# One layer of a hybrid decoder on one core: V of the first token chunk computed in the carry block, transfers issued in earlier or later blocks, and the next chunk's inputs loaded in eight pieces

## What is computed

```
h = rmsnorm(x)
[q | k | v | u | g_att | g_s5] = h @ w_in
att = rmsnorm(diff_attention(q, k, v)) * (1 - lambda_init)      # 8 heads, causal
s5  = y + d * u, y from the diagonal complex recurrence on u   # 64 groups, 64 states each
z   = gelu(s5);  s5o = z * sigmoid(z @ w_glu + b_glu)
x   = x + (sigmoid(g_att) * (att @ w_proj_att) + sigmoid(g_s5) * (s5o @ w_proj_s5)) @ w_out
x   = x + PEER(rmsnorm(x))      # per token 8 heads pick 16 of 16384 experts by top-k
y   = rmsnorm(x)
```

## Time and profile before

| What | Value |
|---|---|
| Runs, median (lowest to highest) | 4465.69 us (4462.35 to 4467.46) |
| The profiled execution's own time | 4462.64 us |
| Its span in the trace | 4460.9 us |
| Its mean granted TensorE clock | 0.908 of full speed |
| PE busy | 3361.5 us, 75% |
| DVE busy | 3039.5 us, 68% |
| ACT busy | 1502.3 us, 34% |
| POOL busy | 1323.9 us, 30% |
| Moved by DMA | 1416.84 MB, mean 318 GB/s |
| of it expert rows gathered by POOL | x1056, queue q0, 1129.94 MB |
| L911 POOL gathers | 1248.5 us |
| L1014 DVE dot products | 1288.9 us |
| L656 PE stationary tiles | 1109.4 us |

### The profile page before, as it was taken

The page is one execution under the profiler, slowest core; times in us unless marked ns, Lnnn a source line. Parts: engine busy times, 40 slices in busy tenths (PEclk is TensorE's granted clock), DMA queues, the critical chain, the costliest instruction groups (busy, mean ns, idle before and its releaser), DMA issues. The chain is left out here.

```text
span 4460.9 us, 43476 instructions
## 1 busy us (share of the span) xinstructions
PE 3361.5 (75%) x13280; PEld 1915.9 (43%) x13280; DVE 3039.5 (68%) x6500; ACT 1502.3 (34%) x3882; POOL 1323.9 (30%) x1168
## 2 busy tenths in 40 slices
PE   7857979787768869877668758877777777777776
PEld 4646666544434444344456634432222222222221
DVE  6473021788888878877776758886676676666664
ACT  2121140333553324254443323223333333333332
POOL 0100000233223333322233323344444444444442
PEclk9878989998879889988888969999999999999999
DMA  3117425998778999966699979899999999999997
GB/s 130 18 3 105 146 86 179 369 394 340 261 271 347 362 383 392 409 211 228 221 364 402 405 266 417 327 412 419 419 418 416 412 413 413 412 412 400 411 407 304
DMA packets 284909, 1416.84 MB, mean 318 GB/s; under 512 B 47459, under 2 KB 88899, under 8 KB 147587
## 3 DMA queue, kind: packets, MB, share of 16 engines
q0 software_dynamic: 159344, 1129.94, 63.5%
q1 hardware_dynamic: 124946, 283.98, 18.7%
q10 hardware_dynamic: 384, 0.13, 0.0%
HBM read 1370.00 MB, written 42.11 MB: 317 GB/s over the span
## 5 line engine op out<-in xcount | busy, mean ns | idle before, releaser
L911 POOL DMA_INDIRECT arena<-in_uv,arena x1056 | 1248.5, 1182 | 2312.9 <-DVE arena L1024 1417.6
L1014 DVE CUSTOM_DVE_ANT_0 arena<-arena 128x1024 f32<-128x1024 f32 x1056 | 1288.9, 1222 | 510.4 <-DMA arena<-in_uv,arena 481.9
L1132 PE MATMUL ps<-arena 128*128 128x512 f32 (+1 forms) x2288 | 1086.6, 620 | 404.3 <-ACT arena L1101 404.3
L656 PE MATMUL ps<-arena 128*128 128x256 f32 (+2 forms) x3456 | 1109.4, 481 | 146.6 <-DMA arena<-in_w_stat 68.3
L656 PEld LDWEIGHTS ps<-arena 128*128 128x128 f32 x3456 | 682.7, 201 | 536.9 <-issue 354.1
L1132 PEld LDWEIGHTS ps<-arena 128*128 128x128 f32 (+1 forms) x2288 | 413.4, 190 | 1076.9 <-ACT arena L1101 629.1
L1024 DVE SCALAR_TENSOR_TENSOR arena<-arena 128x1024 f32<-128x1024 f32 x484 | 618.9, 1279 | 18.7 <-ACT arena L1091 18.7
L1082 ACT ACTIVATE arena<-arena 128x2 f32<-128x2 f32 x528 | 107.2, 203 | 1533.1 <-DVE arena L1014 1514.8
L1091 ACT ACTIVATE arena<-arena 128x1 f32<-128x1 f32 x1056 | 253.4, 287 | 17.7 <-ACT arena L1082 0.5
L1082 ACT ACT_TABLE_LOAD x156 | 200.1, 1283 | 46.0 <-PEq L1260 28.9
L1101 ACT ACTIVATE arena<-ident,arena 128x128 f32<-128x128 f32 x540 | 187.2, 394 | 8.8
(11 more groups left out here) (251 smaller groups left out, 3294.7 us busy)
## 6 DMA issues: line engine op xcount, KB each, us to landing
arena<-in_w_stat SPq DMA_DIRECT2D x216, 512.0 KB, 7.8
arena<-in_cache_k SPq DMA_DIRECT2D x64, 512.0 KB, 10.7
arena<-in_cache_v SPq DMA_DIRECT2D x64, 512.0 KB, 11.5
arena<-in_w_mov SPq DMA_DIRECT2D x14, 2048.0 KB, 14.5
arena<-in_uv,arena POOLq DMA_INDIRECT x1056, 13.1
arena<-in_x SPq DMA_DIRECT2D x16, 512.0 KB, 9.2
arena<-scr_s POOLq DMA_DIRECT2D x64, 128.0 KB, 12.9
scr_s<-arena SPq DMA_DIRECT2D x16, 384.0 KB, 15.2
```

Of the source, the lines that this page charges most:

```text
L656: last = nc.tensor.matmul(ps[:, bank, 0:w], wbuf[m % NWB][:, kc * P:(kc + 1) * P], moving[:, kc, :], start=(kc == 0), stop=(kc == KC - 1))
L911: pool.indirect_dma_start(ring[s % RING], None, dr["uv"], bass.IndirectOffsetOnAxis(ap=idx[:, g % 4, j:j + 1], axis=0)).then_inc(row_in[s ...
L1014: nc.vector.tensor_tensor_reduce(ring[s % RING][:, 0:D], ring[s % RING][:, 0:D], h2r[:, b % 2, :], 1.0, 0.0, ALU.mult, ALU.add, act_in[:, ...
L1132: last = nc.tensor.matmul(ps[0:m, 4 * (b % 2) + c, :], diag[:, n % 4, 0:m], ring[s % RING][:, D + 512 * c:D + 512 * (c + 1)], start=start, ...
```

## The change

- The loads of the u weights are issued at the end of the norm block instead of the start of the next one.
- The seven Toeplitz copies are issued at the start of the carry block instead of the end of the block before. PE waits for them ahead of the samples' outputs.
- V of the first chunk (tokens 0 to 255) is computed in the carry block: SP loads its columns of `hT` back from `scr_h` and the V weights in two halves, the second behind `zs_ready`, since its place holds the samples' z until then. PE does the products behind L522, ACT copies them out, SP stores them, and ACT waits for these stores before the first gelu of the late block. `stage_values` runs for chunks two and three only, and "s5" of the first chunk loads no V weights.
- In the late block DVE's copy of the samples' z stands first instead of behind the states, SP's store of it stands ahead of the samples' states, and the first three weight tiles are issued at the block's start instead of behind the sixth z store.
- `stage_queries` loads the next chunk's z and `hT` in eight pieces of two feature blocks each, two pieces at each of heads 1 to 4, ahead of that head's store of scores, instead of two DMAs at head 2.

```diff
@@ norm block, SP
+                for k in range(2):
+                    sp.dma_start(slab[:, k, :, :].rearrange("p a b -> p (a b)"), dr["w_mov"][k]).then_inc(slab_in[k], 16)
@@ parameter block, SP
-                for k in range(2):
-                    sp.dma_start(slab[:, k, :, :].rearrange("p a b -> p (a b)"), dr["w_mov"][k]).then_inc(slab_in[k], 16)
...
-                sp.wait_ge(toe_zero, 2)
-                for s in range(1, ST8):
-                    sp.dma_start(m_toe[s * CH:(s + 1) * CH, :, s * CH:P],
-                                 kst[:, :, 0:ST8 - s, :].rearrange("p g t c -> p g (t c)")).then_inc(toe_in, 16)
@@ carry block
+        h_v0 = lay(AT_KS + 1664, [KC, 2 * P])
+        w_v0 = [lay(AT_KS + 1664 + 2 * D, [KC, 512]), lay(AT_WS, [KC, 512])]
+        v_st0 = lay(AT_KS + 1664 + 2 * D, [2, D])
-        zs_st = lay(AT_WS + G * P + 256, [KC, NS])
+        zs_st = lay(AT_WS, [KC, NS])
@@ carry block, PE
                 last.then_inc(zs_ready, 1)
+                pe.wait_ge(se_free, GP)
+                for k in range(2):
+                    pe.wait_ge(v0_in[k], 32 - 16 * k)
+                    for b in range(2):
+                        for kc in range(KC):
+                            last = nc.tensor.matmul(ps[:, 2 * k + b, :], h_v0[:, kc, b * P:(b + 1) * P], w_v0[k][:, kc, :],
+                                                    start=(kc == 0), stop=(kc == KC - 1))
+                        last.then_inc(v_ready, 1)
@@ carry block, ACT
+                act.wait_ge(v_ready, 2)
+                for k in range(2):
+                    for b in range(2):
+                        act.wait_ge(v_ready, 2 * k + b + 1)
+                        nc.scalar.activation(v_st0[:, b, 512 * k:512 * (k + 1)], ps[:, 2 * k + b, :], ACT.Copy).then_inc(v_free, 1)
@@ carry block, SP
+                for s in range(1, ST8):
+                    sp.dma_start(m_toe[s * CH:(s + 1) * CH, :, s * CH:P],
+                                 kst[:, :, 0:ST8 - s, :].rearrange("p g t c -> p g (t c)")).then_inc(toe_in, 16)
+                sp.dma_start(h_v0, scr_h.rearrange("p (c t) -> p c t", c=KC)[:, :, 0:2 * P]).then_inc(v0_in[0], 16)
+                for k in range(2):
+                    if k:
+                        sp.wait_ge(zs_ready, 1)
+                    sp.dma_start(w_v0[k].rearrange("p a b -> p (a b)"), dr["w_mov"][2 + k]).then_inc(v0_in[k], 16)
+                sp.wait_ge(v_free, 4)
+                for b in range(2):
+                    sp.dma_start(out["v"][b * P:(b + 1) * P, :], v_st0[:, b, :]).then_inc(v_out[b], 16)
                 sp.wait_ge(rec, N_CARRIED)
@@ late block, SP
+                for m in range(NWB):
+                    load_tile(sp, m)
+                sp.wait_ge(zs_free, 1)
+                sp.dma_start(z_all[:, :, SEQ:T], zs_st).then_inc(zs_out, 16)
                 sp.wait_ge(rec, N_LATE + 8)
...
                     if c == KC - 3:
                         sp.wait_ge(yp_ready, KC)
-                        for m in range(NWB):
-                            load_tile(sp, m)
                         load_hT(sp, 0)
@@ stage_merge, SP
-                        if j in (4, 8):
+                        if j in (4, 8) and (c or fold):
@@ stage_queries, SP
-                        if h == 2 and c + 1 < len(CHUNKS):
-                            load_zT(sp, c + 1)
-                            load_hT(sp, c + 1)
+                        if 1 <= h <= 4 and c + 1 < len(CHUNKS):
+                            for part in (2 * h - 2, 2 * h - 1):
+                                load_next(sp, c + 1, part)
@@ the loop over chunks
-            stage_values(c)
+            if c:
+                stage_values(c)
```

More of the change, by code:

```diff
@@ L112, in hybrid_step @@
         NORM_GROUPS = ((0, 4), (4, TT + 1))
+        slab, slab_in = lay(AT_KS, [2, KC, 512]), [sem(f"slab_in{k}") for k in range(2)]
         def x_rows(t):
@@ L240, in hybrid_step @@
         scr_h = nc.dram_tensor("scr_h", (P, KC * T), F32, kind="Internal").ap()
-        par_in, slab_in = sem("par_in"), [sem(f"slab_in{k}") for k in range(2)]
+        par_in = sem("par_in")
         u_ready, u_free = sem("u_ready"), sem("u_free")
@@ L723, in _ @@
                 z_g = z_tok.rearrange("p t (g c) -> p t g c", c=CH)
+                for b in range(2):
+                    act.wait_ge(v_out[b], 16)
                 for q in range(KC):
```

32 lines of the change are left out of this document (16 added, 16 removed).

## The result

The changed kernel takes **4410.25 us** (median of 4 runs, 4402.33 to 4415.35) against 4464.02 us (4458.99 to 4467.46, 4 runs) beside it: ratio 0.9878, 95% interval 0.9865 to 0.9892, 54 us. A second set of runs of the same two kernels, later, gave 4412.47 us and 0.9886 (0.9871 to 0.9900). Over both sets the changed kernel is 52 us (1.2%) faster. The profiled execution took 4413.32 us, its span 4411.5 us, the mean granted clock is 0.910.

A forecast was written before the change was run, and what follows sets the result against it. Up to 846 us each block waits for one engine, then the DMA engines are nearly full. Terms of 6.5, 10.1, 29.4, 0.8, 3, 3.5, 1 and 8 sum to 62.3 us off the 4465.69 median: 4403 us, range 4387 to 4422.

The forecast's parts named there:

- u weights and Toeplitz copies: Start: earlier u weights let PE start sooner, 6.5 us; moved Toeplitz copies let the carry begin sooner, 10.1 us.
- Late block and first glu: Late block 3 us (range -6 to 13.8), the least certain term; first glu starting earlier, 3.5 us (1 to 7).
- V, and the tile wait in "s5": First chunk: V hidden in the carry's free PE time, 29.4 us; a tile wait in "s5" gone, 0.8 us.
- Pieces, first chunk: First chunk's query stage: PE's tile wait goes, but DVE's chain sets the end; 1 us (-3 to 7).
- Pieces, second chunk: Second chunk's query stage: scores no longer queue behind two large loads; 8 us (0 to 18.6).
- The regime: Engine-bound blocks up to 846 us, DMA engines nearly full after; a front gain arrives unless a later block turns it back.
- Rival (b): Late block: both of PE's waits go, 13.8 us in place of 3, 4393 us; chance 0.13.
- The second bound: Second chunk's query stage: of DVE's 18.59 us wait, 8.2 us of transfer must remain, so 10.4 us less.
- rival (c): Pieces bring nothing or the late block loses, each 9 us less gain: 4412 us, with both 4421; chance 0.20.

The follow-up runs named there:

- the start alone: The kernel before with only the u weight loads moved to the norm block's end and the Toeplitz copies to the carry block's start: 4447.03 us, ratio 0.9962.
- V in its stage: The changed kernel with V of the first chunk back in its own stage behind "s5", its weights loaded there again: 4436.56 us, ratio 0.9947.
- the scores first: The changed kernel with the prompt's state stored in rows and each head's scores store issued ahead of the pieces: 4405.74 us, ratio 0.9868.
- after without the pieces: The changed kernel with the next chunk's z and `hT` loaded by two DMAs at head 2 again: ratio 0.9889.
- with rows alone: The changed kernel with the prompt's final state copied to rows and stored as 128 pieces of 256 bytes, not 8192 of 4: 4398.78 us, ratio 0.9863.
- V in its stage with rows: The changed kernel with V of the first chunk back in its stage and the prompt's state stored in rows of 256 bytes: 4430.37 us in one run.
- before with the pieces: The kernel before with only the next chunk's z and `hT` loaded in eight pieces, two at each of heads 1 to 4: ratio 0.9990.
- before with rows: The kernel before with only the prompt's final state stored in rows of 256 bytes instead of single elements: 4459.58 us, ratio 0.9990.
- the late tiles: The changed kernel with the first glu's three weight tiles issued behind the sixth z store again, ahead of `hT`: 4407.93 us, ratio 0.9878.

## Why the prediction was right, and where not

The forecast was 4403 us, a gain of 62.3; the median was 4410.25, inside the range, and the gain over both sets 52 us. So the forecast was 10 us too high in all; V and the start, three quarters of it, were right term by term. The table takes each term from all executions that have the edit against all that lack it, since one pair misleads.

| Term | Predicted | Measured |
|---|---|---|
| u weights and Toeplitz copies | 16.6 | 18.4 (carry starts at 222.9 in four executions, 204.5 in ten) |
| Late block and first glu | 6.5 | 3.1 (212.0 in four, 208.9 in three, from carry to the end of glu) |
| V, and the tile wait in "s5" | 30.2 | 30.4 (86.9 and 87.25 against 56.6) |
| Pieces, first chunk | 1 | 0 |
| Pieces, second chunk | 8 | 4.7 |
| Sum | 62.3 | 56.6 |

**What held.** *The start.* PE's first u product came at 34.62 (forecast 34.9), and DVE covered it as said. The two terms were a little small: PE ended the parameter block 7.9 us earlier on the mean, not 6.5, so the 1.2 us taken off for a lower clock did not show at the block's end, and the copies gave the other 10.5 (forecast 10.1). The carry starts at 202.0 to 203.1 or at 205.1 to 206.5 us, and the time of the transposes L335 tells which: 10.0 to 10.2 us in the four early ones, 11.6 to 11.9 in the six late ones. *V.* Hidden whole, at the price forecast, with 9 us between its last product (289.6) and DVE's end (298.6), where 8 were forecast. *The regime.* A lead in front arrives at the end nearly whole: 17 of 20 us for the start alone, 29 for V, where the traces show 31.8 from the carry's start to the attention (296.1 us with V in its stage, 264.3 the mean of the changed kernel's two). The reason given was too simple, though: the DMA engines are not nearly full all the way behind 846 us. In the second chunk's attention stage their share is 0.74 and they move 263 GB/s.

**What failed first: the late block, 3 us.** Split at DVE's first and last operation of the late block, the 3.1 us of the table are 0.3 gained ahead of it, 2.0 lost within it (77.5 us on the mean of four, 79.5 of three) and 4.8 gained from there to the end of the first glu (37.1 and 32.4), where 3.5 were forecast. Single executions lie between 75.0 and 83.6 us before and between 76.0 and 81.3 after, so the late block's loss is not told from nothing, and no more is 3.1 from 6.5. Two steps failed. The waits were priced from one execution, and the wait behind the tiles was named as an argument but given no price: in after PE's 7.09 and 6.72 us have become 1.66 and 0.42, and DVE's third copy waits 15.35 us for a z store in their place. PE's 6.72 us stop was 1.42 us in the second execution of before and 1.70 us in the kernel with the start alone, whose late block is the same; DVE waited 7.47 and 8.24 us for a z store there instead. That this one stop ended within 0.2 us of the small store's landing was chance: in those two it ended 2.0 and 2.9 us ahead of it. The reading of its cause was right even so: the small writes hold both the load of instructions and the landings, as their removal showed. The prediction's reason for preferring 3 us over a full gain, that the tiles stand ahead of the z stores, proved to be the other half: 6 us of DVE's 15.35 are theirs. Rival (b), both of PE's waits gone and the time with them, did not come by this change, since DVE's wait took their place; it came by storing the state in rows, and was worth 9.5 us in front and 8.5 at the end (0.9863 against 0.9882, whose intervals overlap; about 6.5 over the three changed kernels with rows against the four sets without), where rival (b) had stood 10.8 us over the forecast.

The rule of the Trainium skill (DMA: Bandwidth & Descriptors, Queues, rings and completion order), that an engine takes turns between queue rows packet by packet, does not account for this alone: one packet of instructions took 10.1 us of an engine beside the small writes and 1.5 us without them (7.5 to 13.3 us in nine traces, less than 1.5 in five). The same page (Back-pressure in remote DMA) says, of transfers between cores, that stalled writes stall the other queues of the engine too. That would fit what the traces here show, for writes of 4 bytes to DRAM; no run here tests it.

**What failed second: the pieces, 8 us.** The step took 54.6 MB at 415 GB/s; its window of 140 us was 4 us longer than the stage. The stage in fact moved 389 GB/s for 135.75 us before, 52.8 MB, and 410 GB/s for 130.82 us after, 53.6 MB. At 52.8 MB and 410 it would have been 7 us; 0.8 MB more, 2 us, were moved within the stage. So the rate was set 5 GB/s too high, and the bytes were held fixed where they were not. The second bound read DVE's wait as the loss: 10.5 us of it went and 8.10 stayed, but the stage gained only 4.9, and with the scores first the wait was gone and the stage no shorter. In the first chunk the price of 1 us was nothing, as rival (c) had it.

**The 15 us that seemed to be given back.** In the first pair of traces the lead fell from 64.1 us at the first attention to 59.5 at the second chunk's, to 53.7 behind it, rose to 58.4 by the query stage with the pieces, and fell to 53.9 by the end of the last chunk's attention and to 49.4 in the rest. The second chunk's attention stage took 5.7 us, and it is no effect of the change: it lasted 286.7 to 287.3 us in before, the start alone, V in its stage, the two after without the pieces or with rows alone, and V in its stage with rows (286.8), and 291.6 to 292.8 in before with the pieces, before with rows, both executions of after, the late tiles and the scores first; 283.9 and 289.8 were seen as well. Each side has variants of both kernels. The means are 288.4 us over five executions of before and its variants and 289.6 over nine of after and its variants. The length goes with the granted clock: its mean over the stage is 0.82 or 0.83 in the eight traces where the stage took 283.9 to 289.8 us and 0.80 or 0.81 in the six where it took 291.6 to 292.8. These are before and, 5.4 us longer, before with the pieces (columns as in the earlier trace rows); after has 0.80 too, after without the pieces 0.82:

```profile
1059.16:1346.16 287.00, 198.90 (x816) 126.86 (x817) 229.26 (x449) 145.13 (x334) 70.66 (x57) 0.82 0.74 263
```

```profile
1054.25:1346.66 292.41, 204.95 (x816) 131.05 (x817) 229.50 (x449) 145.31 (x334) 71.22 (x57) 0.80 0.73 257
```

The products are the same, DVE and ACT are busy as long, and PE is busy 6 us longer. Nearly all of it arises in the first 127 us of the stage. Why the clock is granted later in one execution than in another stays open, and no run changed the clock alone. The last chunk's attention stage (764 to 774 us) and the last block (1624 to 1630 us) spread as widely, with means that differ by about 1 us each between the two sides. Of the 64.1 us themselves some 8 were before's unlucky late block (218.0 us against 209.9, the mean of the other three), which stayed in that pair to the end. Between the sum of the means, 56.6, and the end, 52, there remain 4 to 5 us. The ratios' own intervals reach 6 us either way, so whether a few per cent of a lead are lost in the DMA-full part was not settled.

## What to carry to other kernels

Ask of each stage start which transfer it waits for and whether its source was ready a block earlier; ask of each engine's free time whether a later stage with ready inputs fits into it. Both are read from idle times, and here both were worth what these said (18.4 us for 16.6, 30.4 for 30.2). But an idle time of one engine is a gain only if no other engine's wait stands behind it: price that one too. Never leave a store of thousands of 4-byte elements beside other transfers: here one copy that made it contiguous freed SP, the landings behind it and the load of instructions. And before pricing a wait of a few microseconds, look for it in a second execution.

## What the runs showed that was not expected

- The store of 8192 single elements, behind which the tiles were issued, held SP for 31.51 us at the next issues; stored in rows of 256 bytes, 2.58 us. One load of instructions took 10.1 us of one engine beside it and 1.5 us without.
- The clock differs by execution at the same place. In the first 10 us of the late block PE is busy throughout in all fourteen traces. Behind 43.5 to 44.5 us of idle time the clock there was 0.50 in four of them, the lower level, and 0.76 to 0.83 in three; behind 13.4 to 15.4 us it was 0.50 in five and 0.76 to 0.77 in two. So the length of the idle time does not decide it alone, nor do the small writes (0.50 in seven of nine traces with them and in two of five without). These are before with the pieces (44.05 us idle) and the changed kernel with the state in rows (15.00 us):

```profile
324.49:334.49 10.00, 10.00 (x73) 8.14 (x74) 9.86 (x14) 1.97 (x16) 0.00 (x0) 0.76 1.65 1
```

```profile
304.64:314.64 10.00, 10.00 (x74) 8.13 (x75) 9.86 (x14) 1.97 (x16) 0.00 (x0) 0.77 0.16 42
```

- That first difference costs nothing here: the second execution of before has 51 products at 0.50 in the same 10 us, yet in all five executions of before and its variants PE comes to its first transposes of z 32.45 to 32.48 us behind its first product, since it waits there for DVE (7.09 to 14.61 us). A rise of the clock counts where PE is what the others wait for, as in the two executions of after, where it moved the late block by 5 us, as much as several of the terms of the sum.
